# Cache pages: the page numbers of the next group are loaded into registers ahead of the wait for its ring slot

## The chip, the cores and the metric

The kernel runs on one core of one Trainium2 chip. The metric is the time of one execution on the device in microseconds (us); the kernel before takes 1488.07 us, the median of three runs from 1487.55 to 1489.52. A profile is one more execution, recorded instruction by instruction, with a time of its own.

## The reference

It is one step of a decoder layer: a half-step SwiGLU feed-forward network (ffa), a mixing block, a second feed-forward network (ffb), a layer norm after each. 512 prompt tokens and 8 decoding sequences of one token each go through the same weights. The part that matters here is the attention of the 8 decoding tokens over their past, which lies in a paged cache. A table of page numbers says which pages belong to which sequence:

```python
k_past = cache_k[l][page_table].reshape(DB, past, DA_HEADS, 2, DA_QK)
v_past = cache_v[l][page_table].reshape(DB, past, DA_HEADS, DA_V)
lp = jnp.einsum('bqhmd,bkhmd->bhmqk', q, k_past)       # logits of the past
attn = p[:, :, 0] - lam * p[:, :, 1]                   # two softmax maps per head
o = jnp.einsum('bhqk,bkhe->bqhe', attn[..., :P], v_past) + ...
```

Eight sequences with 16 pages of 128 positions each give 128 pages of keys and 128 pages of values. A page is 128 rows of 512 float32 values, 256 KB. The same block also holds the prompt's attention and an RWKV-7 recurrence (projections, triangular inverses, state products), which is other work for the same engines.

## The kernel before

The instructions of every engine are written out by hand, and semaphores order them. TensorE (PE), VectorE (DVE), ScalarE (ACT) and GpSimd (POOL) compute. SyncE (SP) issues nearly all DMA transfers, in the order of its program, and everything behind a wait on SP waits too.

The mixing block interleaves three strands on TensorE: the prompt's attention, the RWKV-7 work and the decoding tokens' pages. The pages come in 64 groups of GROUP = 4: groups 0 to 31 (N_GROUPS = 32) are keys, groups 32 to 63 are values. A key group is used by `decode_keys_tensor` (matmuls of L1063, four of 128x512), a value group by `decode_values_tensor` (L1126). Both first wait for all four pages of the group, and signal `pages_used` with their last matmul. Their places between the other matmuls are fixed.

The buffers are a ring of RING_GROUPS = 2 slots, `cache_pages0` and `cache_pages1`. `page_group(k)` on SP fills slot k % 2. From group 2 on it first waits until TensorE has used group k - 2, which lay in that slot. For each of the four pages it then loads the page number from the table in SBUF (`TABLE`, in profiles `page_ids`) into a register of SP with `value_load` (L1962: the instructions TENSOR_LOAD, FUSED_REGOPS and SEQ_ASSERT) and issues the transfer whose address is computed from it (L1964: FUSED_REGOPS, MOVE and DMA_DIRECT2D). Four loads and four issues thus alternate, all behind the wait. Between page groups SP also issues the last blocks of the input projection's weights (`input_block`, L1971), the outputs `v_out` (L2006), `k_out` (L2009) and `shift_out` (L2013), and one block of weights behind group 28 (L2018). Behind group 63, SP waits for the end of the mixing block and streams the weights of the output projection (L239) and of ffb.

ACT issues a few transfers of its own: 256 KB pieces of the recurrent state, in (L1640) and out (L1633).

Of the kernel before, what the change touches and what calls it, by code (L numbers as in the profile page):

```python
# [16 lines left out]
D_MODEL, SEQ, DEC = 1024, 512, 8  # L17
# [10 lines left out]
PAGES = PAST // PAGE  # L28
POOL = 160
# [28 lines left out]
GROUP, RING_GROUPS = 4, 2  # L58
# [53 lines left out]
def layer(nc, x_in, gu_a, down_a, w_in, w_out, gu_b, down_b, consts, vecs, lams, lora, g2,  # L112
# [17 lines left out]
    with ctx:  # L130
        def sb(name, shape, dt=f32, to=ctx):
            return to.enter_context(nc.sbuf_tensor(name, shape, dt))

        def sem(name):
            return ctx.enter_context(nc.semaphore(name))
# [58 lines left out]
        TABLE = sb("page_ids", [1, DEC * PAGES], i32)  # L194
# [13 lines left out]
        def g(name):  # L208

            if name not in sems:  # L210
                sems[name] = sem(name)
            return sems[name]
# [21 lines left out]
        def load_weights(sp, pr, i, src):  # L234
            for b, (k0, nk, _, _, _) in enumerate(pr.body):

                wait_from_one(sp, split_lo, 2 * (pr.block(i, b) - 1))
                slot = pr.raw_slot(b)
                sp.dma_start(RAW[slot][:, 0:nk, :], src(i, b)).then_inc(raw_ready[slot], 16)  # L239
# [37 lines left out]
        def multiply_woven(pe, slabs, seq, hi, lo, ready):  # L277

            order, seen = [], {}
            for n, (k, t) in enumerate(seq):  # L280
                pr, i, b = slabs[k]
                _, nk, sets, _, _ = pr.body[b // 2]
                s, slot = sets[b % 2], pr.slot(b)
                if k not in seen:
                    seen[k] = 0
                    pe.wait_ge(split_lo, pr.slab(i, b) + 1)
                    wait_from_one(pe, acc_free[s], pr.set_uses(i, b))
                if t not in order:
                    order.append(t)
                    pe.wait_ge(ready[0], ready[1] + len(order))  # L290
                seen[k] += 1
                for m, (w, x) in enumerate(((WH, hi), (WH, lo), (WL, hi))):
                    for a in range(2):
                        mm = nc.tensor.matmul(acc[s][:, a, 0:HALF], w[slot][:, t, :], x[:, t, HALF * a:HALF * a + HALF],  # L294
                                              start=seen[k] == 1 and m == 0, stop=seen[k] == nk and m == 2)
                if seen[k] == nk:
                    mm.then_inc(slab_used, 1)
# [331 lines left out]
        N_LEVELS = len(LEVELS) - 1  # L629
        JOBS = ring_order()  # L630
        JOB_AT = {name: n for n, (name, _, _) in enumerate(JOBS)}
        READER = {name: reader for name, reader, _ in JOBS}
        READS, FIRST_BANK, BEFORE = {}, {}, {}
        reads, at, holds = {"v": 0, "s": 0}, 0, [None] * 4
        for name, reader, banks in JOBS:
            reads[reader] += 1
            READS[name] = reads[reader]
            if banks == 2 and at % 2:
                at = (at + 1) % 4
# [4 lines left out]
            at = (at + banks) % 4  # L644
# [382 lines left out]
        N_GROUPS = QUARTERS * DEC  # L1027
# [910 lines left out]
        def _(sp):  # L1938
# [10 lines left out]
            def down(w):  # L1949
# [3 lines left out]
                        .rearrange("a p (k n) -> p (a k) n", n=2 * P)  # L1953
                return src

            def page_group(k):
                if k >= RING_GROUPS:
                    sp.wait_ge(g("pages_used"), k - RING_GROUPS + 1)
                slot, v = k % RING_GROUPS, k - N_GROUPS
                for n in range(GROUP):  # L1960
                    at = k % DEC * PAGES + k // DEC * GROUP + n if v < 0 else (2 * n + v % 2) * PAGES + v // 2
                    pid = sp.value_load(TABLE[0:1, at:at + 1], min_val=0, max_val=POOL - 1)  # L1962
                    cache = cache_k if v < 0 else cache_v
                    sp.dma_start(PG[slot][:, n, :], cache[bass.ds(pid, 1), :, :].rearrange("a p n -> (a p) n"))\  # L1964
                        .then_inc(g(f"pages_in{slot}"), 16)

            def input_block(n):
                pr, i, k = slab_of(2 * n)
                wait_from_one(sp, split_lo, 2 * (pr.block(i, k // 2) - 1))
                slot = pr.raw_slot(k // 2)  # L1970
                sp.dma_start(RAW[slot][:, :, :], w_in[ORDER[n][0] // 2, :, :].rearrange("p (k n) -> p k n", n=2 * P))\  # L1971
                    .then_inc(raw_ready[slot], 16)
# [21 lines left out]
            for n in range(6, 11):  # L1994
                input_block(n)
            sp.wait_ge(g("table_in"), 16)
            page_group(0)
            page_group(1)
            input_block(11)
            page_group(2)  # L2000
            input_block(12)
            page_group(3)
# [209 lines left out]
```

## Time and profile before

| | |
|---|---|
| median of three runs | 1488.07 us (1487.55 to 1489.52) |
| the profiled execution: its time, its span | 1481.32 us, 1479.5 us |
| TensorE busy, VectorE, ScalarE, GpSimd | 88%, 37%, 28%, 6% of the span |
| first page issued, last page group used | 534.5 us, 952.6 us from the span's start |
| page transfers | 256 of 256 KB, 3.0 us each from issue to landing |

The span is the time from the first to the last instruction of the program in the profile. Times inside the profile are counted from its start. PE is a matmul, PEld the load of its stationary operand; SPq are instructions of SP's sequencer. "Landing" is the moment at which the transfer's semaphore has its full count. A wait on an engine is counted as idle time in front of the instruction that waits.

### The profile page before, as it was taken

What the parts mean: (1) busy time and instruction counts of PE and PEld (TensorE: products, weight loads), DVE (VectorE), ACT (ScalarE), POOL (GpSimd) and SP (SyncE); (2) the same over time, 40 slices, a digit from 0 to 9 for tenths busy, and PEclk for the clock granted to TensorE, in tenths of its full rate; (3) what the DMA queues carried; (4) which work ended last, traced back from release to release, by engine and by line L of the source; (5) the groups of instructions that cost most, each with busy time, mean ns of one, the idle gap of its engine ahead of it and who ended that gap; (6) DMA issues with size and microseconds to landing.
All of it is one profiled execution on the core that took longest, in us unless ns stands there. A gap on an engine that the chain in (4) does not pass through costs nothing.

```text
span 1479.5 us, 30154 instructions
## 1 busy us (share of the span) xinstructions
PE 1296.7 (88%) x12636; PEld 1161.2 (78%) x12636; DVE 554.0 (37%) x787; ACT 421.1 (28%) x637; POOL 94.8 (6%) x92
## 2 busy tenths in 40 slices
PE   6999999999969977977768777779699999999995
PEld 6999999999958976854436334369599999989994
DVE  3332332223364552235522423275633333322224
ACT  4322222211234521126612313132332222221113
POOL 0000000000100021002410001002000000000000
PEclk9999999999979989999978889789899999999998
DMA  5222222223225233664574567533122322213211
GB/s 201 86 92 107 85 85 71 79 79 96 80 95 196 78 128 105 204 197 138 166 218 142 169 205 213 179 151 136 58 86 86 109 88 85 78 57 100 78 57 58
DMA packets 55963, 174.62 MB, mean 118 GB/s; under 512 B 7105, under 2 KB 7362, under 8 KB 47298
## 3 DMA queue, kind: packets, MB, share of 16 engines
q1 hardware_dynamic: 53282, 168.84, 34.2%
q10 hardware_dynamic: 2592, 4.52, 0.8%
q8 instruction: 64, 1.05, 0.3%
q14 instruction: 25, 0.20, 0.0%
HBM read 163.58 MB, written 9.76 MB: 117 GB/s over the span
## 4 chain that ended last, share of the span: by engine, by line
PE 37%; DVE 5%; DMA 4%; SPq 4%; ACT 3%; issue 2%; DVEq 0%; ACTq 0%
PE acc L271 26%; DMA cache_pages<-in_cache_v 2%; SPq L1962 2%; SPq L1964 2%; PE acc L294 2%; PE acc L1126 1%; PE acc L391 1%; DMA x_lo<-trunk_lo 1%; DVE weights_lo L254 1%; PE acc L717 1%; PE acc L1294 1%; PE acc L1397 1%; PE acc L1063 1%; PE acc L1317 1%; PE acc L1200 1%
## 5 line engine op out<-in xcount | busy, mean ns | idle before, releaser
L254 DVE TENSOR_TENSOR weights_lo<-weights_raw,weights_hi 128x1024 fp32r<-128x1024 f32 (+2 forms) x186 | 207.1, 1122 | 525.1 <-ACT weights_hi L247 525.0
L271 PE MATMUL acc<-x_hi,weights_hi 128*128 128x260 f32 x1728 | 354.1, 286 | 17.3 <-DVE x_lo L2079 11.6
L271 PE MATMUL acc<-x_lo,weights_hi 128*128 128x260 f32 x1728 | 350.6, 285 | 0.0
L271 PE MATMUL acc<-x_hi,weights_lo 128*128 128x260 f32 x1728 | 350.6, 285 | 0.0
L247 ACT ACTIVATE weights_hi<-weights_raw 128x1024 fp32r<-128x1024 f32 (+2 forms) x186 | 178.5, 966 | 593.7 <-PE acc L271 558.3
L271 PEld LDWEIGHTS acc<-x_hi,weights_hi 128*128 128x128 f32 x1728 | 270.2, 191 | 26.4 <-issue 25.7
L271 PEld LDWEIGHTS acc<-x_hi,weights_lo 128*128 128x128 f32 x1728 | 269.1, 190 | 0.0
L271 PEld LDWEIGHTS acc<-x_lo,weights_hi 128*128 128x128 f32 x1728 | 268.9, 190 | 0.0
L271 PE MATMUL acc<-hidden_hi,weights_hi 128*128 128x260 f32 x704 | 144.3, 287 | 12.4 <-DVE weights_lo L254 12.4
L271 PE MATMUL acc<-hidden_hi,weights_lo 128*128 128x260 f32 x704 | 143.5, 285 | 0.0
L271 PE MATMUL acc<-hidden_lo,weights_hi 128*128 128x260 f32 x704 | 143.4, 286 | 0.0
L271 PEld LDWEIGHTS acc<-hidden_hi,weights_hi 128*128 128x128 f32 x704 | 110.4, 192 | 13.2 <-issue 13.2
L271 PEld LDWEIGHTS acc<-hidden_lo,weights_hi 128*128 128x128 f32 x704 | 110.6, 191 | 0.0
L271 PEld LDWEIGHTS acc<-hidden_hi,weights_lo 128*128 128x128 f32 x704 | 110.4, 191 | 0.0
L1126 PE MATMUL acc<-cache_pages,query_columns 128*8 128x512 f32 x256 | 40.6, 711 | 30.6 <-DMA cache_pages<-in_cache_v 30.5
L322 ACT ACTIVATE hidden_hi<-scratch 128x520 f32 (+1 forms) x44 | 28.1, 639 | 101.8 <-DVE scratch L333 101.8
L1063 PE MATMUL acc<-cache_pages,query_columns 128*32 128x512 f32 x256 | 38.9, 684 | 15.1 <-DMA cache_pages<-in_cache_k 13.7
L404 POOL TENSOR_TENSOR scratch<-y_sum 128x520 f32<-128x520 f32 x3 | 4.8, 1591 | 725.5 <-DVE y_sum L350 725.5
L336 DVE TENSOR_TENSOR hidden_lo<-scratch,hidden_hi 128x520 f32 (+1 forms) x44 | 30.8, 700 | 38.9 <-ACT hidden_hi L322 38.9
L333 DVE TENSOR_TENSOR scratch<-scratch,acc 128x520 f32<-128x520 f32 x44 | 30.3, 689 | 33.3 <-PE acc L271 33.3
L347 DVE SCALAR_TENSOR_TENSOR y_sum<-x_hi,acc 128x520 f32 (+1 forms) x24 | 16.6, 691 | 62.9 <-PE acc L271 57.7
L391 PE MATMUL acc<-scratch,mean_weights 128*128 128x260 f32 x96 | 30.1, 482 | 11.0 <-ACT scratch L416 11.0
(286 smaller groups left out, 1302.8 us busy)
## 6 DMA issues: line engine op xcount, KB each, us to landing
cache_pages<-in_cache_k SPq DMA_DIRECT2D x128, 256.0 KB, 3.0
cache_pages<-in_cache_v SPq DMA_DIRECT2D x128, 256.0 KB, 3.0
weights_raw<-in_gate_up_a SPq DMA_DIRECT2D x22, 1024.0 KB, 4.8
weights_raw<-in_gate_up_b SPq DMA_DIRECT2D x22, 1024.0 KB, 4.8
weights_raw<-in_w_in SPq DMA_DIRECT2D x13, 1024.0 KB, 4.8
weights_raw<-in_down_a SPq DMA_DIRECT2D x8, 768.0 KB, 4.2
weights_raw<-in_down_b SPq DMA_DIRECT2D x8, 768.0 KB, 4.2
weights_raw<-in_down_a SPq DMA_DIRECT2D x8, 640.0 KB, 3.8
```

The lines of the kernel that those rows point to most:

```text
L247: nc.scalar.activation(WH[pr.slot(k)][:, 0:nk, :], RAW[slot][:, 0:nk, P * (k % 2):P * (k % 2) + P], ACT.Copy).then_inc(split_hi, 1)
L254: nc.vector.tensor_tensor(WL[pr.slot(k)][:, 0:nk, :], RAW[slot][:, 0:nk, P * (k % 2):P * (k % 2) + P], WH[pr.slot(k)][:, 0:nk, :].bitcast( ...
L271: mm = nc.tensor.matmul(acc[s][:, a, 0:HALF], w[slot][:, t, :], x[:, k0 + t, HALF * a:HALF * a + HALF], start=begins and t == tiles[0] and ...
L294: mm = nc.tensor.matmul(acc[s][:, a, 0:HALF], w[slot][:, t, :], x[:, t, HALF * a:HALF * a + HALF], start=seen[k] == 1 and m == 0, stop=see ...
L322: nc.scalar.activation(HH[:, bass.ds(2 * (i - 1) + k - 2, 1), :], SCR[:, k:k + 1, :], ACT.Copy).then_inc(h_hi, 1)
L333: dve.tensor_tensor(halves(SCR[:, k, :]), halves(SCR[:, k - 2, :]), accv(k), ALU.mult).then_inc(hidden, 1)
L336: dve.tensor_tensor(HL[:, bass.ds(c, 1), :], SCR[:, k:k + 1, :], HH[:, bass.ds(c, 1), :].bitcast(f32), ALU.subtract).then_inc(acc_free[k], 1)
L391: mm = nc.tensor.matmul(acc[1][:, a, 0:HALF], MEAN[:, :], SCR[:, 2 + c % 2, HALF * a:HALF * a + HALF], start=c == 0, stop=c == DC - 1)
L1063: mm = nc.tensor.matmul(bank(DECODE_BANK)[32 * h:32 * h + 32, :], QZ[:, h, b, :], PG[k % RING_GROUPS][:, :, P * h:P * h + P], start=b == 0 ...
L1126: mm = nc.tensor.matmul(bank(DECODE_BANK)[32 * j:32 * j + 8, :], WZ[:, n, 8 * b:8 * b + 8], PG[k % RING_GROUPS][:, j, :], start=False, sto ...
L1962: pid = sp.value_load(TABLE[0:1, at:at + 1], min_val=0, max_val=POOL - 1)
L1964: sp.dma_start(PG[slot][:, n, :], cache[bass.ds(pid, 1), :, :].rearrange("a p n -> (a p) n"))\
```

## The change

`page_group(k)` no longer loads page numbers between its transfers. A new helper, `page_ids(k)`, loads the four numbers of group k into four registers and keeps them in the Python dictionary `ids`. `page_group(k)` waits for its slot, issues four transfers in a row from the registers kept, and then calls `page_ids(k + 1)`. So the loads of a group stand in SP's program behind the transfers of the group before it, ahead of whatever SP does between the two groups. Group 0 loads its own numbers first. After group 63 nothing is loaded.

```diff
+            ids = {}
+
+            def page_ids(k):
+
+                v = k - N_GROUPS
+                at = [k % DEC * PAGES + k // DEC * GROUP + n if v < 0 else (2 * n + v % 2) * PAGES + v // 2 for n in range(GROUP)]
+                ids[k] = [sp.value_load(TABLE[0:1, n:n + 1], min_val=0, max_val=POOL - 1) for n in at]
+
             def page_group(k):
+                if k not in ids:
+                    page_ids(k)
                 if k >= RING_GROUPS:
                     sp.wait_ge(g("pages_used"), k - RING_GROUPS + 1)
-                slot, v = k % RING_GROUPS, k - N_GROUPS
-                for n in range(GROUP):
-                    at = k % DEC * PAGES + k // DEC * GROUP + n if v < 0 else (2 * n + v % 2) * PAGES + v // 2
-                    pid = sp.value_load(TABLE[0:1, at:at + 1], min_val=0, max_val=POOL - 1)
-                    cache = cache_k if v < 0 else cache_v
+                slot, cache = k % RING_GROUPS, cache_k if k < N_GROUPS else cache_v
+                for n, pid in enumerate(ids.pop(k)):
                     sp.dma_start(PG[slot][:, n, :], cache[bass.ds(pid, 1), :, :].rearrange("a p n -> (a p) n"))\
                         .then_inc(g(f"pages_in{slot}"), 16)
+                if k + 1 < 2 * N_GROUPS:
+                    page_ids(k + 1)
```

The number of instructions of SP is the same, 1095 rows of the program before and after, and no other engine's program changes. In the lists below, one row is one instruction or several equal ones; "ISA" rows are SP's register instructions, and lines below L1962 have moved: L1964 of before is L1971 of after, and L1971 of before is L1980 of after.

Before, on SP, at group 3 (behind the last block of the input projection's weights), the wait for the slot stands ahead of the first load:

```order
L1971 DMA weights_raw<-in_w_in 128x2048 [waits split_lo]
L1962 TENSOR_LOAD page_ids [waits pages_used]
L1962 ISA x2
L1964 ISA
L1964 DMA cache_pages<-in_cache_k 128x512
L1962 TENSOR_LOAD page_ids
L1962 ISA x2
L1964 ISA
L1964 DMA cache_pages<-in_cache_k 128x512
```

After, on SP, at the same place, the last of group 3's four loads stands ahead of the weights, and the wait stands ahead of four transfers with no load between them:

```order
L1962 TENSOR_LOAD page_ids
L1962 ISA x2
L1980 DMA weights_raw<-in_w_in 128x2048 [waits split_lo]
L1971 ISA [waits pages_used]
L1971 DMA cache_pages<-in_cache_k 128x512
L1971 ISA
L1971 DMA cache_pages<-in_cache_k 128x512
L1971 ISA
L1971 DMA cache_pages<-in_cache_k 128x512
L1971 ISA
L1971 DMA cache_pages<-in_cache_k 128x512
L1962 TENSOR_LOAD page_ids
```

The wait has moved from a load to the first instruction of a transfer, and four loads that stood behind it now stand ahead of it.

Before, on SP, the start of the stretch, where group 0 needs no slot and waits only for the table:

```order
L1962 TENSOR_LOAD page_ids [waits table_in]
L1962 ISA x2
L1964 ISA
L1964 DMA cache_pages<-in_cache_k 128x512
L1962 TENSOR_LOAD page_ids
```

After, on SP, the same place:

```order
L1962 TENSOR_LOAD page_ids [waits table_in]
L1962 ISA x2
L1962 TENSOR_LOAD page_ids
L1962 ISA x2
L1962 TENSOR_LOAD page_ids
L1962 ISA x2
L1962 TENSOR_LOAD page_ids
L1962 ISA x2
L1971 ISA
L1971 DMA cache_pages<-in_cache_k 128x512
```

Here the first transfer has moved behind three more loads.

## Rows read from the trace of the kernel before

**Rows 1.** The page of the profile: busy tenths in 40 slices of the span.

```profile
PE   6999999999969977977768777779699999999995
...
DMA  5222222223225233664574567533122322213211
```

**Rows 2.** Waits of TensorE (PE) on pages: us in total, times, longest.

```profile
PE acc L1063 <- DMA cache_pages<-in_cache_k: 13.7, 6, 4.7
...
PE acc L1126 <- DMA cache_pages<-in_cache_v: 30.5, 16, 4.9
```

**Rows 3.** The chain that ended last, 740 to 953 us, by line.

```profile
by line: DMA cache_pages<-in_cache_v 15.4%; SPq L1962 14.9%; SPq L1964 12.1%; issue 10.9%; PE acc L1126 10.1%; PE acc L1397 3.9%; PE acc L1104 3.5%; DMA cache_pages<-in_cache_k 2.7%; PE acc L1317 2.7%; PE acc L1294 2.5%; PE acc L1063 2.3%; 
```

**Rows 4.** The same chain, pieces in order of time: start us, us, what.

```profile
756.70 2.78 DMA cache_pages<-in_cache_k
...
881.88 0.27 SPq L1962
882.60 0.33 SPq L1964
...
885.86 2.92 DMA cache_pages<-in_cache_v
888.83 1.04 PE acc L1126 x8
...
944.06 2.70 DMA cache_pages<-in_cache_v
```

**Rows 5.** Timeline of TensorE: its wait for the pages of six groups, in brackets.

```profile
647.66 0.73 PE L1063 MATMUL acc<-cache_pages,query_columns 128*32 128x512 f32 x4 [4.73 <-DMA cache_pages<-in_cache_k]
...
806.47 1.04 PE L1126 MATMUL acc<-cache_pages,query_columns 128*8 128x512 f32 x8 [0.89 <-DMA cache_pages<-in_cache_v]
...
828.25 1.23 PE L1126 MATMUL acc<-cache_pages,query_columns 128*8 128x512 f32 x8 [2.99 <-DMA cache_pages<-in_cache_v]
...
865.54 1.04 PE L1126 MATMUL acc<-cache_pages,query_columns 128*8 128x512 f32 x4 [4.90 <-DMA cache_pages<-in_cache_v]
...
903.72 1.60 PE L1126 MATMUL acc<-cache_pages,query_columns 128*8 128x512 f32 x8 [3.28 <-DMA cache_pages<-in_cache_v]
...
942.51 1.90 PE L1126 MATMUL acc<-cache_pages,query_columns 128*8 128x512 f32 x8 [2.09 <-DMA cache_pages<-in_cache_v]
```

**Rows 6.** L1962, L1964, L1063: duration ns min/median/max, first and last start us.

```profile
L1962 SPq TENSOR_LOAD <-page_ids x256: 262/268/967, 533.6 to 947.7; - x128
L1962 SPq FUSED_REGOPS  x256: 152/152/177, 534.1 to 948.0; - x128
L1962 SPq SEQ_ASSERT  x256: 18/18/33, 534.3 to 948.2; - x128
...
L1964 SPq FUSED_REGOPS  x256: 37/37/42, 534.4 to 948.3; - x128
...
L1063 PE MATMUL acc<-cache_pages,query_columns x256: 589/617/1062, 562.0 to 769.5; 128*32 128x512 f32 x128
...
L1964 SPq MOVE cache_pages<-in_cache_k x128: 29/29/38, 534.5 to 765.4; - x128
```

**Rows 7.** Timeline of SP: a run of 12 page issues, start us, us.

```profile
753.43 12.40 SPq L1964 DMA_DIRECT2D cache_pages<-in_cache_k  x12
```

**Rows 8.** SP's waits for slots, 862 to 953 us: total, times, longest.

```profile
SPq L1962 <- PE acc L1126: 5.9, 7, 2.0
```

**Rows 9.** The page of the profile: issues, KB each, us to landing.

```profile
cache_pages<-in_cache_v SPq DMA_DIRECT2D x128, 256.0 KB, 3.0
weights_raw<-in_gate_up_a SPq DMA_DIRECT2D x22, 1024.0 KB, 4.8
```

**Rows 10.** DMA packets of 534 to 542 us, then of 920 to 950 us.

```profile
DMA packets 881, 2.42 MB, mean 302 GB/s; under 512 B 95, under 2 KB 95, under 8 KB 751
...
DMA packets 3743, 6.88 MB, mean 229 GB/s; under 512 B 416, under 2 KB 416, under 8 KB 3738
```

**Rows 11.** L1962's loads from 594 to 606.5 us, beside the stores of k and v.

```profile
L1962 SPq TENSOR_LOAD <-page_ids x8: 265/450/967, 595.1 to 605.7; - x8
```

**Rows 12.** Stretch 939 to 944 us: busy us of the engines, clock, DMA share, GB/s.

```profile
939.00:944.00 5.00, 2.91 (x20) 0.63 (x16) 0.50 (x2) 0.00 (x0) 0.00 (x0) 0.50 0.81 255
```

## The prediction

> **What bounds the kernel now.** I read the page first. TensorE is busy at 9 tenths over most of the span, and dips to 6 to 8 tenths only in the middle, where the mixing block runs and where the DMA engines are busiest [rows 1]. The rest of the kernel is feed-forward networks, which the change doesn't touch. So the question is what TensorE waits for in the middle.
>
> The list of waits says that 44.2 us of its idle time end with the landing of a page: 13.7 us in 6 waits for key pages and 30.5 us in 16 waits for value pages [rows 2]. Idle time counts only where it lies on the path, so I then read the chain of work that ended last. From 740 to 953 us, 18.1% of the chain is page transfers, and 27.0% is SP loading numbers and issuing (14.9% and 12.1%) [rows 3]. Of 213 us that is 57.5 us; a group shows in these two lines with about 4 x 0.84 = 3.35 us (below), so some 17 groups stand on the chain with their whole issuing. The transfers stand on it 12 times, the first at 756.70, the last at 944.06 us [rows 4]. Before 740 us the chain has no page piece: there it runs through ScalarE, VectorE and TensorE.
>
> One passage shows the pattern: TensorE has used a group, SP loads the first number at 881.88, issues the fourth page at 885.86, the page lands 2.92 us later, and TensorE goes on at 888.83 [rows 4]. From the free slot to the use it is 6.95 us, of which 3.98 us lie before the fourth issue.
>
> **The change part by part.** *The spacing on SP.* Twelve issues in a row take 12.40 us, the last being 0.33 long, so one page costs SP (12.40 - 0.33) / 11 = 1.10 us, and a group 4.4 us [rows 7]. The load part is 268 + 152 + 18 = 438 ns [rows 6], the issue part 37 + 29 + 333 = 399 ns, of which 333 ns are the transfer's own instruction [rows 4, 6]. The two sum to 837 ns, so 260 ns are gaps between six instructions, 43 ns each. With three gaps each, a load costs 0.57 us and an issue 0.53 us.
>
> *After the change* the first issue starts 0.14 us behind the free slot (37 + 29 ns and gaps) and not 0.72, and the fourth at 0.14 + 3 x 0.53 = 1.73 us and not 3.98. The four loads, 2.3 us, come behind. Where SP then waits for a slot anyway, they are hidden; where it doesn't, a group still costs it 4.4 us. The change takes nothing off SP's work: it moves the issues to the front of SP's turn.
>
> *How much of this the landing keeps.* Four pages issued within 1.6 us are 1 MB at once. Pages have never been issued so closely in the trace, so I bound it. From below: one weight transfer of 1,024 KB lands 4.8 us after its issue [rows 9], which gives 0.14 + 4.8 = 4.9 us behind the free slot. From above: at the mean 229 GB/s of the late stretch [rows 10] a page of 262 KB takes 1.14 us, and the fourth lands at 0.14 + 3.0 + 3 x 1.14 = 6.6 us. But that rate is one of pages issued 1.1 us apart, so it may only be what was asked for. Where page transfers met a weight transfer in flight, the rate was 302 GB/s [rows 10], 0.87 us a page; a weight transfer that comes alone moves its last 768 KB in 4.8 - 3.0 = 1.8 us, 0.60 us a page [rows 9]. I take 0.75, between these two: 0.14 + 3.0 + 2.25 = 5.4 us. Against 6.95 us that is **1.5 us per passage**, with ends of 0.35 and 2.0.
>
> The Trainium skill ("DMA: Bandwidth & Descriptors", section "Latency and other measured facts") gives a floor of about 600 ns for a load of a register from a tensor. The trace disagrees: the median of 256 loads is 268 ns [rows 6]. By the page the four loads would take 1.3 us more out of the path and a passage would shrink by up to that much more; by the row the sum stays as it is.
>
> *How many passages.* A wait can give back no more than it has, and in a stretch where SP's 4.4 us per group set the pace the earlier issue is gained once, not per group. In order of time: the end of the keys (748 to 769 us, five waits in a row) once, 1.5; the wait of 0.89 us at 806.47, 0.9; the wait of 2.99 at 828.25, 1.5; one near 843 us, 1.5; 4.90 at 865.54, 1.5; the run of three from 880 to 889, once, 1.5; 3.28 at 903.72, 1.5; and the last stretch, from 924 to 952, once, 1.5 [rows 5]. That is 7 x 1.5 + 0.9 = 11.4 us. In the last 91 us SP waited only 5.9 us in all [rows 8], so no more than about 5.9 + 1.5 us can come from there; I count 4.5.
>
> *The group at 647.66* waited 4.73 us [rows 5], as its pages landed late among transfers of states that ScalarE issues. There the four issues now come before those. Up to 3 us are gained at that point, but before 740 us the chain runs through other engines, so I let 0.6 us of it last. The sum is **12 us**.
>
> *What else moves.* The four loads of the next group now stand ahead of whatever SP does between two groups: two blocks of the input projection's weights, the stores of v, k and the last rows, one block of weights behind group 28. None of these comes later for it, since the turn before them lost as many loads as it got. Only group 0 has four loads more than it had in its turn: its first page is issued 3 x 0.57 = 1.7 us later, its fourth at the same time (4 x 0.57 + 1.73 = 4.0 us), and SP reaches the weights behind group 1 some 2.3 us later. TensorE uses the first page at 562.0 [rows 6], 27 us behind the first issue of before, and the weights wait for VectorE's signal anyhow. If both covers were gone it would cost 2.3 us once. The new wait stands ahead of the transfers; behind it is nothing but SP's own program, as before. Behind group 63 nothing is loaded, so the output projection's weights come no later.
>
> Against its own execution the sum is 1481.32 - 12 = 1469.3 us. That execution was 6.75 us faster than the median, so for the median I take 1488.07 - 12 = **1476 us**.
>
> **The rivals.** *A. The transfers set the landing.* If four pages at once get no more than the 229 GB/s of the late stretch [rows 10], a passage gains 0.35 us and 8 to 9 of them give 3 us: 1485 us. For it: the DMA engines are busy 0.81 of the time at 939 to 944 us, with 255 GB/s [rows 12]. Against it: the 302 GB/s, and weight transfers that land 1 MB in 4.8 us. The Trainium skill ("DMA: Bandwidth & Descriptors", section "Bandwidth") has a transfer of 1 MB, issued from GpSimd, at 6.15 us; by that page a passage would take 0.14 + 6.15 = 6.3 us and the sum would be about 5.5 us; the row of 4.8 us disagrees with it for this kernel.
>
> *B. Other engines take over.* What TensorE no longer waits for pages it waits for ScalarE and VectorE, as it does before 740 us. If only half of the passages last, 6 us remain: 1482 us. Against it: 45% of the chain from 740 us on is SP and pages, and the steps between two passages are mostly TensorE's own [rows 3]. What is late next at these places is TensorE's own matmuls.
>
> *C. It gets slower: the loads behind four transfers are long.* The longest load took 967 ns, and the eight from 594 to 606.5 us have a median of 450 ns, against 268 [rows 11]. Each long one stood behind a page issue while a store of k or v was in flight. If four transfers in a row have this effect on the loads behind them, SP's turn grows, and it counts at each of the some 17 groups on the chain. It is even with the gain at 12 / 17 = 0.7 us per group. With two loads of each group as long as the worst there, some 1.0 us per group, it is 17 - 12 = +5 us: 1493 us. Against it: the other loads stood behind page issues too, with up to three pages in flight, and stayed at 268 ns; the long ones stood beside stores, which read SBUF.
>
> *D. More than forecast.* TensorE's clock stands at 0.50 of full, its lower level of 1.2 GHz, from 939 to 944 us, and a group's matmuls take 1.90 us there [rows 5, 12] against 1.04 us elsewhere. Up to then TensorE had been idle in 2 of 5 us. If the shorter waits bring the clock back for six groups, that is 6 x 0.86 = 5 us more: 1471 us.
>
> **How the numbers follow.** Forecast 0.60, A 0.11, B 0.12, C 0.08, D 0.09. The forecast's own ends are its passages at 1.1 and 1.9 us: 1479 and 1472 us. About 0.2%, 3 us, is what a measurement can tell from no change, so faster means below 1485.1. That holds for the forecast, for B, for D and for a few of A's cases: 0.82. A's others and the mild cases of C are the same: 0.11. Slower is 0.07. The range takes in D with a somewhat faster transfer, 1468, and B and A up to 1485; outside are C above and 1 in 10 at the lower end.
>
> **What would show it.** In the changed profile, four issues stand 0.53 us apart, four loads behind them are still at 268 ns with a turn of 4.4 us where SP doesn't wait, and the fourth page lands 5.4 us behind the slot's release. TensorE's waits for pages fall from 44 to about 30 us, and SP's loads are gone from most of the chain. The median time from issue to landing must rise above 3.0, since pages queue behind each other; if it rises to about 4.2 for the fourth, A has come true. I am wrong if the loads grow (C), or if TensorE's waits shrink and the time doesn't (B).

## The result, and the profile after

The changed kernel takes 1480.09 us, the median of five runs (1475.03 to 1483.22), against 1489.07 us before (five runs, 1487.55 to 1490.58). The ratio is 0.9933, with a 95% interval of 0.9913 to 0.9953. It is faster by 9.0 us where 12 were forecast, and 1480.09 lies in the range of 1468 to 1485.

The two profiled executions say the opposite: 1483.22 us for the changed kernel, the slowest of its five runs, and 1481.32 us for the kernel before, which is faster than every run of it that was timed without a profile. So each kernel was profiled once more among the experiments (after_again, 1473.44 us; before_again, 1486.31 us). Below, a main reading counts only if both profiles of a kernel show it.

The page of the changed kernel, busy tenths in 40 slices, beside [rows 1]:

```profile
PE   6999999999969977978768768688699999999995
...
DMA  5222222223225233654564566533122322213211
```

TensorE's dips in the middle are still there: of the 40 slices six differ, three of them by a tenth up and three down.

TensorE's waits for pages in the changed kernel, as in [rows 2] (us in total, times, longest):

```profile
PE acc L1126 <- DMA cache_pages<-in_cache_v: 29.9, 15, 3.5
...
PE acc L1063 <- DMA cache_pages<-in_cache_k: 10.2, 3, 4.2
```

The total is 40.1 us, and 38.4 in the second profile; it was 44.2, and 46.0 in the second profile of the kernel before. What has shrunk most is the longest wait for values: 4.9 and 4.7 us in the two profiles before, 3.5 in both now.

SP's instructions for the page groups, from the list of the changed kernel's tiles and lines, beside [rows 6] and [rows 9] (duration ns min/median/max, first and last start in us; then us from issue to landing):

```profile
L1962 SPq TENSOR_LOAD <-page_ids x256: 260/266/936, 532.7 to 945.1; - x128
...
L1971 SPq DMA_DIRECT2D cache_pages<-in_cache_k x128: 332/333/2621, 535.3 to 766.2; - x128
...
DMA to landing us min/median/max: 2.5/3.5/6.6
```

The loads are as long as before. The transfers take longer from issue to landing, 3.5 us for 3.0, since four of them now stand in the queues together.

One passage of the changed kernel, from the chain that ended last (start us, us, what):

```profile
897.43 1.02 PE acc L1126 x8
...
898.61 0.33 SPq L1971
899.13 0.33 SPq L1971
899.68 0.33 SPq L1971
900.20 0.33 SPq L1971
...
900.88 0.27 SPq L1962
```

TensorE's last matmul on the old group ends at 898.45. The four issues follow, 0.52 to 0.55 us apart, and the loads for the next group stand behind them. The fourth issue is 1.75 us behind the free slot; in [rows 4] it took 3.98 us. The fourth page landed at 904.28 and TensorE went on at 904.32, 5.9 us behind the free slot where [rows 4] have 6.95 (counted there from the first load).

The chain of the changed kernel from 740 to 953 us, by line, first and second profile:

```profile
by line: SPq L1971 12.4%; DMA cache_pages<-in_cache_v 12.3%; issue 10.9%; PE acc L1126 9.2%; SPq L1962 8.4%; PE acc L1309 5.5%; PE acc L1294 4.5%; PE acc L1397 4.3%; PE acc L1317 4.0%; PE acc L1104 3.5%; PE acc L1063 2.9%; PE acc L1200 2.2%
```

```profile
by line: SPq L1971 16.2%; SPq L1962 12.2%; issue 10.5%; DMA cache_pages<-in_cache_v 10.1%; PE acc L1126 8.0%; PE acc L1317 4.0%; PE acc L1294 3.9%; PE acc L717 3.5%; PE acc L1104 3.5%; PE acc L1397 3.0%; PE acc L1284 2.3%; PE acc L1200 2.2%
```

Value transfers stood on the chain with 15.4% [rows 3], 14.1% in the second profile of before, and stand there with 12.3 and 10.1%. But SP's loads are still on it, with 8.4 and 12.2%.

### The profile page after: what moved, and what is told of

The parts are those of the page before. It is cut to its first block, busy times and chain, and to the rows that moved or that the text cites. A ratio compares the mean times of both kernels' runs of the same rounds, so it can differ in the third digit from the quotient of the medians.

```text
span 1481.4 us, 30154 instructions
## 1 busy us (share of the span) xinstructions
PE 1301.0 (88%) x12636; PEld 1166.8 (79%) x12636; DVE 554.5 (37%) x787; ACT 422.0 (28%) x637; POOL 94.1 (6%) x92
## 4 chain that ended last, share of the span: by engine, by line
PE 77%; DVE 7%; ACT 5%; DMA 4%; issue 3%; SPq 3%; ACTq 0%; DVEq 0%
PE acc L271 61%; PE acc L294 3%; SPq L1971 2%; DMA cache_pages<-in_cache_v 2%; PE acc L1063 2%; PE acc L391 2%; DVE weights_lo L254 1%; PE acc L717 1%; PE acc L1126 1%; SPq L1962 1%; PE acc L1317 1%; PE acc L1294 1%; DMA x_lo<-trunk_lo 1%; PE acc L1309 1%; PE acc L1397 1%
## 5 line engine op out<-in xcount | busy, mean ns | idle before, releaser
L1063 PE MATMUL acc<-cache_pages,query_columns 128*32 128x512 f32 x256 | 38.6, 678 | 11.6 <-DMA cache_pages<-in_cache_k 10.2
```

What stands on the lines that cost most here:

```text
L1063: mm = nc.tensor.matmul(bank(DECODE_BANK)[32 * h:32 * h + 32, :], QZ[:, h, b, :], PG[k % RING_GROUPS][:, :, P * h:P * h + P], start=b == 0 ...
```

## The experiments

The theory L: a passage through a free slot got shorter by what the fourth landing got earlier, and apart from that SP's turn per group (4.4 us, unchanged) still sets the pace. The rivals are those of the prediction, above all B (other engines take over, so how far the loads are moved makes no difference) and A (the transfers alone set the landing). In some of the expectations, theory B is another one: that issues close to each other are what counts. Theory C is there a gain that lies in TensorE's clock or in chance stops.

Five measures come from the traces by one rule. Over the groups in which SP waited for the slot, the time runs from the end of the last matmul on the slot's old group to the first issue, the fourth issue and the fourth landing; the table has the medians. They are over the groups whose first issue directly follows that end (18 to 52 of them). Most of these groups are key groups; the value groups alone give 7.12 and 7.25 us for the fourth landing in the two profiles before (18 and 19 groups), 5.87 and 6.18 with the change (9 each). SP's turn is the lower quartile of the times from a value group's first issue to the next one's. In most kernels that is a group where SP didn't wait, and the shortest turns are within 0.02 us of it. In the three kernels without the range check SP waits at most groups and the quartile is too long: the shortest turns are 3.23 us in no_assert_before, 3.26 in no_assert and 2.95 in multi_load.

The ratio is that of a kernel to the kernel before as it ran beside it, whose median was 1486.99, 1488.62 or 1489.14 us.

| kernel | ratio to before (95%) | slot to 1st issue | to 4th issue | to 4th landing | turn |
|---|---|---|---|---|---|
| before, again | 1.0015 (0.9996 to 1.0035) | 0.78 | 4.04 | 7.18 | 4.37 |
| the change, again | 0.994 (0.992 to 0.9961) | 0.21 | 1.76 | 6.16 | 4.29 |
| one_ahead | 0.9953 (0.9936 to 0.997) | 0.20 | 3.47 | 6.53 | 4.35 |
| two_ahead | 0.9933 (0.9907 to 0.9959) | 0.21 | 2.91 | 6.31 | 4.35 |
| no_assert_before | 0.9912 (0.988 to 0.9945) | 0.50 | 2.92 | 6.66 | 3.65 |
| no_assert | 0.988 (0.986 to 0.99) | 0.20 | 1.76 | 6.13 | 3.32 |
| double_loads | 1.0101 (1.008 to 1.0122) | 0.21 | 1.76 | 6.14 | 5.38 |
| half_before | 0.9919 (0.9894 to 0.9944) | 0.77 | 4.04 | 6.25 | 4.37 |
| half_after | 0.9837 (0.9814 to 0.9861) | 0.21 | 1.76 | 4.15 | 4.29 |
| multi_load | 0.9874 (0.9842 to 0.9906) | 0.20 | 1.75 | 6.23 | 3.46 |

All times are us. The first profiles of the two kernels give 7.03 (before) and 6.05 (after) for the fourth landing.

### How far ahead: one number, two, all four

In each of these kernels a function `ahead(k)` says how many of a group's four numbers are loaded behind the transfers of the group before it. The others are loaded between the transfers, as before.

```diff
-                for n, pid in enumerate(ids.pop(k)):
+                for n in range(GROUP):
+                    pid = ids.pop((k, n)) if (k, n) in ids else page_id(k, n)
```

one_ahead has `return 1`:

> Only the first of the next group's four numbers is loaded ahead of the wait; the other three are loaded between the transfers, as before. SP's turn is as long as before. Theory L (what counts is the time from the free slot to the landing of the fourth page): the first issue comes 0.57 us earlier, the fourth too (at 3.4 us in place of 4.0), the fourth page lands 0.6 us earlier, and nine passages give 5 us: ratio 0.9965. Theory B (close issues are what helps, or hurts): spacing is unchanged at 1.1 us, so nothing: 1.000. Theory C (the gain is in TensorE's clock or in when executions happen to stall): no order between this run, the one with two ahead and the full change.

Measured: 1479.97 us, ratio 0.9953 (0.9936 to 0.997). two_ahead has `return 2`:

> Two of the four numbers are loaded ahead. Theory L: the fourth issue comes at 2.9 us behind the free slot; with 2.9 us to land it would be there at 5.8 us, and as the transfers themselves held the fourth page to about 6.0 us in the full change, this has nearly all of the full gain: 8 us, ratio 0.9945. If instead the gain grows with each load moved, half of it: 0.9965. Theory B: a third of the full gain, since two of the issues are close.

Measured: 1474.61 us, ratio 0.9933 (0.9907 to 0.9959).

The fourth landing moves step by step, from 7.0 or 7.2 us to 6.5, 6.3 and then 6.05 or 6.16 us with all four ahead. The time moves with it at first. L had expected 0.9965 and 0.9945; both lie in the intervals, and so one number ahead can't be told from what L expected, nor two ahead from four. That only close issues count (1.000 for one number ahead) is excluded. The fourth issue counts less than its own shift: from two to four ahead it comes 1.15 us earlier (2.91 to 1.76), but the landing only 0.15 to 0.26 us. By then the pages queue behind each other, as the half pages below show.

### Keys or values

values_only has `return 0 if k < N_GROUPS else 4`:

> The numbers are loaded ahead for the value groups (32 to 63) alone; the key groups are as before. Theory L: seven of the nine passages lie there, so about 6.5 to 7 us of the 9: ratio 0.9955. If the gain is the group at 647 us, where the states come in between, or the end of the keys, this run shows under 3 us: 0.998 or more.

Measured: 1480.94 us, ratio 0.9955 (0.9938 to 0.9973), as expected. keys_only has `return 4 if k < N_GROUPS else 0`:

> The numbers are loaded ahead for the key groups (0 to 31) alone. Theory L: two of the nine passages, and the value groups alone had 6.5 us: 2 us, ratio 0.9985. If it has more than 4 us, the parts don't add up, and the gain of the value groups alone must have had another source.

Measured: 1489.15 us, ratio 0.9993 (0.9974 to 1.0012): nothing that can be told from no change, though a gain up to 3.9 us is inside the interval, and so are the 2 us of L. The two halves multiply to 0.9948, which is in the intervals of the whole. The gain that can be measured is in the values.

### SP's turn, shorter and longer

no_assert loads the numbers without the check of their range, so FUSED_REGOPS and SEQ_ASSERT (152 + 18 ns and their gaps) go, four times per group; no_assert_before does the same with no number ahead.

```diff
-                ids[k] = [sp.value_load(TABLE[0:1, n:n + 1], min_val=0, max_val=POOL - 1) for n in at]
+                return sp.value_load(TABLE[0:1, at:at + 1])
```

> As the changed kernel, with the numbers loaded without the check that they lie in range (two instructions less per page): SP's turn goes from 4.35 to about 3.3 us. This leaves out the check only. Theory L with SP as the pace of the late stretches: beyond the change's gain another 3 to 4 us, ratio 0.991. If the transfers are the pace (1 MB needs 5.8 us to land and two groups overlap), a shorter turn brings nothing: 0.994 as the change.

> The order of before (load, issue, load, issue, all behind the wait), with the numbers loaded without the check of their range. This leaves out the check only. SP's turn is 3.3 us, the fourth issue comes at about 2.85 us behind the free slot. Theory L with the pace: the fourth page lands at about 5.8 to 6.0 us, as in the changed kernel, and the turn is as short as in the run with the change and no check; so it has the gain of that run, or 1 to 2 us less: ratio 0.989. Theory B (close issues, loads out of the way of the wait): without moved loads it has only what the shorter turn gives, that is the difference between that run and the change: 0.995.

Measured: 1469.30 us, ratio 0.988 (0.986 to 0.99), and 1477.19 us, ratio 0.9912 (0.988 to 0.9945). A turn that is 1.0 us shorter (the shortest ones are 4.28 and 3.26 us) gains 8 to 9 us beyond the change (0.9933 or 0.994 to 0.988), where 3 to 4 were expected: this was a miss by size. The two edits together give more than the change alone. Whether they give more than no_assert_before, or less than the product of the two single ratios (0.9853), can't be told: the interval of no_assert_before is 0.0033 wide to each side. It takes in L's 0.989 and, just, not the 0.995 of the theory of close issues. Now SP goes partly off the chain. The chain of no_assert from 740 to 938 us, by line, and SP's waits for slots with values:

```profile
by line: DMA cache_pages<-in_cache_v 12.5%; SPq L1978 11.7%; PE acc L1126 10.6%; issue 9.7%; PE acc L1309 7.0%; PE acc L1317 4.3%; SPq L1964 3.8%; PE acc L1294 3.8%; PE acc L1104 3.7%; PE acc L1063 3.7%; PE acc L1397 3.0%; PE acc L1284 2.5%
```

```profile
SPq L1978 <- PE acc L1126: 52.8, 17, 21.5
```

Loads (L1964 there) and issues (L1978) fall to 15.5% together, against 20.8 and 28.4% in the two profiles of the change. SP waits for TensorE in 17 groups of values; with the change alone it waits in 9 and 7.

double_loads goes the other way: two loads more per group, whose numbers nobody uses, behind the transfers.

```diff
                 if k + 1 < 2 * N_GROUPS:
                     page_ids(k + 1)
+                    for n in range(2):
+                        page_id(k + 1, n)
```

> The changed kernel with two more loads of a number, unused, behind each group's four: SP's turn is 5.5 us in place of 4.35, the issues and the landings stay as in the change. Theory L with SP as the pace: at some 17 groups the turn is on the path, so 17 x 1.14 = 19 us are lost and 9 gained: ratio 1.007. If the turn hides behind TensorE and only the landing counts, it stays at 0.994.

Measured: 1502.69 us, ratio 1.0101 (1.008 to 1.0122). That is slower than before the change, though the fourth page lands 6.14 us behind the free slot, as early as with the change. Its chain from 740 to 972 us, and SP's waits for slots with values from 795 to 970 us:

```profile
by line: SPq L1964 30.3%; SPq L1978 23.1%; issue 16.5%; DMA cache_pages<-in_cache_v 5.1%; PE acc L1104 3.2%; PE acc L1126 2.6%; DMA cache_pages<-in_cache_k 1.8%; PE acc L1397 1.6%; PE acc L1063 1.3%; PE acc L1294 1.3%; PE acc L1284 1.3%; PE
```

```profile
SPq L1978 <- PE acc L1126: 21.3, 2, 16.7
```

SP waits in 2 groups only, and 53.4% of the chain is SP. From the change (0.994) to this kernel (1.0101) are 24 us for a turn that is 1.09 us longer: it counts about 22 times. L had expected 17 times and 1.007, which is just outside the interval, on the side of too little. So L's second half holds: where TensorE waits for SP's turn, the turn's length counts. That moving loads within such a turn gives nothing is argued; no kernel has the long turn in the order of before.

### Half of each page

half_before and half_after move only 256 of the 512 columns of each page (the first two groups apart), in the order of before and of the change. TensorE's matmuls are the same. The other half of the slot keeps older data, so these two kernels leave out half of the past and return wrong values for it; they are for measuring only. Of the edit, the line of the transfer:

```diff
+                    sp.dma_start(PG[slot][:, n, 0:512 if k < 2 else 256], cache[bass.ds(pid, 1), :, 0:512 if k < 2 else 256].rearrange("a p n -> (a p) n"))\
```

> Each page transfer from group 2 on brings only the first 256 of the 512 columns; the other half of the slot keeps older data, so the attention over the past is computed from wrong values, with the same matmuls. Order of before. The transfers are half as large, so the fourth lands perhaps 0.3 us earlier; SP's turn and spacing are as before. Theory L: the fourth issue at 4.0 us sets the landing, so hardly anything is gained: 2 to 4 us, ratio 0.998.

> The same half pages with the changed order: the fourth issue comes 2.25 us earlier than in the half pages of before. Theory L with transfers that hold the fourth page back: now nothing holds it, so nine passages keep 2 us and not 0.95: 17 to 19 us against before, ratio 0.988. If the spacing of the landings (1.2 us from the second to the third and from the third to the fourth) comes from something else than the amount of data, a fixed time per transfer for example, it stays at 0.993.

Measured: 1475.48 us, ratio 0.9919 (0.9894 to 0.9944), and 1462.51 us, ratio 0.9837 (0.9814 to 0.9861). Both were misses by size. The first was expected to gain 2 to 4 us, since its issues are 1.1 us apart as before; it gains 12, as each transfer is some 0.8 us shorter by itself. The list of tiles has it for half_before:

```profile
DMA to landing us min/median/max: 1.9/2.2/4.4
```

So a passage ends 0.8 to 0.9 us earlier there, and gains like the change without any change of order. The second was expected to gain 17 to 19 us and gains 24. Its fourth page lands 2.9 to 3.0 us earlier than before, so the gain is about 8 us for each us, against some 9 in the change. The medians of the landings of pages 1 to 4, behind the first issue of their group:

| kernel | 1st | 2nd | 3rd | 4th |
|---|---|---|---|---|
| before | 2.96 | 4.06 | 5.26 | 6.29 |
| after | 2.79 | 3.57 | 4.74 | 5.86 |
| the change, again | 2.77 | 3.60 | 4.70 | 5.95 |
| half_before | 2.19 | 3.25 | 4.39 | 5.48 |
| half_after | 2.17 | 2.73 | 3.28 | 3.99 |

With whole pages, issued 0.53 us apart, the third and the fourth land 1.10 to 1.25 us behind the one before. With half pages they land 0.55 and 0.71 us apart, little more than their issues. Nothing differs but the size, so in the change the fourth landing is set by the transfers' size, and no longer by SP's spacing alone. Whether it is the bytes or the size of the packets isn't told apart: a half page has rows of 1 KB where a whole one has 2 KB.

### The two kernels again

> The changed kernel once more, on the chip of this call, and for a second profile. Theory L: 0.993 to 0.994. In its profile TensorE's waits for pages are below those of before; the idle pieces of TensorE that no wait explains (6 pieces over 0.9 us, 10.1 us, against 3 with 3.6 us in the first pair of profiles) are of single executions and are at 3 to 6 pieces here too.

> The kernel before against itself: 1.000, with an interval that shows what five rounds can tell. Its first profile was of an execution of 1481 us, faster than all timed ones (1483 to 1494); this one should be near 1487, with more unexplained idle pieces or a lower clock of TensorE than the first.

Measured: 1477.49 us, ratio 0.994 (0.992 to 0.9961), and 1487.92 us, ratio 1.0015 (0.9996 to 1.0035). With their profiles the pair can be compared along its length. From TensorE's first page group to its last it is 396.9 us in before_again and 385.6 us in after_again; the first profiles had 390.7 and 392.0. The waits of TensorE for three value groups in before_again, from its timeline:

```profile
845.87 1.90 PE L1126 MATMUL acc<-cache_pages,query_columns 128*8 128x512 f32 x8 [3.70 <-DMA cache_pages<-in_cache_v]
...
865.82 1.89 PE L1126 MATMUL acc<-cache_pages,query_columns 128*8 128x512 f32 x8 [4.65 <-DMA cache_pages<-in_cache_v]
...
942.05 1.89 PE L1126 MATMUL acc<-cache_pages,query_columns 128*8 128x512 f32 x8 [4.63 <-DMA cache_pages<-in_cache_v]
```

and for the same groups in after_again:

```profile
841.64 1.90 PE L1126 MATMUL acc<-cache_pages,query_columns 128*8 128x512 f32 x8 [2.86 <-DMA cache_pages<-in_cache_v]
...
860.41 1.04 PE L1126 MATMUL acc<-cache_pages,query_columns 128*8 128x512 f32 x8 [3.50 <-DMA cache_pages<-in_cache_v]
...
937.20 1.90 PE L1126 MATMUL acc<-cache_pages,query_columns 128*8 128x512 f32 x8 [3.15 <-DMA cache_pages<-in_cache_v]
```

The waits are 0.84, 1.15 and 1.48 us shorter, which is about the size of the earlier landing (1.0 us). The second group also runs its eight matmuls in 1.04 us and not 1.89: TensorE's clock is back at 2.4 GHz there. In after_again 10 of the 64 groups take over 1.5 us for their matmuls, that is, they run mostly at the lower clock of 1.2 GHz; in before_again it is 16 (11 and 14 in the first profiles).

Where the first profile of the changed kernel lost its gain shows on its TensorE, against the kernel before, long before the values. The timeline of after:

```profile
663.32 0.33 PE L1294 MATMUL acc<-inverse,t_turned 64*64 64x64 f32 x4 [1.94 <-issue]
```

and the stretches from 660 to 670 us, of after and then of before (us, busy us of PE, PEld, DVE, ACT, POOL, granted clock, DMA share, GB/s):

```profile
660.00:670.00 10.00, 7.18 (x94) 5.16 (x94) 2.35 (x4) 2.77 (x4) 0.00 (x0) 0.69 0.10 32
```

```profile
660.00:670.00 10.00, 7.66 (x194) 5.79 (x194) 4.42 (x8) 4.50 (x7) 0.00 (x0) 1.00 0.40 119
```

TensorE stopped for 1.94 us with no wait on another engine or a page, and the mean clock of the stretch is 0.69 and not 1.00. Two key groups that are 10.6 us apart before came 14.6 us apart here. In after_again the same stop is 1.35 us long and they are 12.0 us apart. Stops over 0.9 us that the profile calls "issue" add up, in the mixing block, to 3.6 and 6.2 us in the two profiles before and 10.1 and 7.4 us with the change.

These stops are not accidents of single executions. In all 14 profiles they stand before the same seven matmuls of TensorE's program; one takes 0.94 us every time, and the other six vary from nothing to 2.5 us. What comes in front of those six shows among the DMA packets, from 660.9 to 662 us of after:

```profile
q8 instruction: 1, 0.02, 5.1%
```

This is one packet of 16 KB on a queue for instructions, from 660.98 to 661.88 us, and TensorE goes on at 663.32. In each of the 48 stops over 0.9 us at the six places, such a packet ended 1.0 to 1.6 us before TensorE went on. So TensorE most likely waits there for its own next instructions; no run holds this apart from other causes.

Does the change make these stops longer? Three of the six places are in the stretch of the keys (663, 750 and 755 us). Together they take 5.8 and 3.6 us in the two profiles of the change, and 4.0 to 4.9 in the other four kernels that issue four whole key pages at once. In the eight profiles that don't, they take 0.5 to 2.9 us (1.0 and 2.5 before). At the three places in the stretch of the values there is no such difference (3.4 and 3.7 us with the change, 3.5 and 4.0 before). This is a likely reason why keys_only gains nothing, but it isn't shown: behind its stops before_again waits for key pages anyway, and no run changes the stops alone.

### One load for four numbers

multi_load builds on the change and reads a group's four numbers with one load into four registers (a row of four for keys, every 32nd number for values), without the check of their range.

```diff
-                ids[k] = [sp.value_load(TABLE[0:1, n:n + 1], min_val=0, max_val=POOL - 1) for n in at]
+                _, ids[k] = nc.values_load_multi_w_load_instructions(
+                    these, engines=[sp.engine if hasattr(sp, "engine") else sp], min_val=0, max_val=POOL - 1,
+                    skip_runtime_bounds_check_because="the page table holds numbers of the pool")
```

> As the changed kernel, with one load instruction for the four registers of a group (the four numbers lie at one spacing in the table) and without the check of their range, which is all that is left out. SP's turn falls from 4.35 to between 2.5 us (a load costs the same for four registers) and 3.3 us (200 ns and more for each). Theory L with the pace: at least the gain of the run without the check, ratio 0.985 to 0.988. If the landing (5.9 us) and TensorE's own use of the slot now set the pace, nothing beyond 0.988.

Measured: 1468.99 us, ratio 0.9874 (0.9842 to 0.9906), the same as no_assert within their intervals. The list of the load's line, for all, then up to 767.5 us (the keys' numbers), then from there to 940 us (the values'):

```profile
L1966 SPq TENSOR_LOAD <-page_ids x64: 295/850/984, 534.1 to 932.9; - x64
...
L1966 SPq TENSOR_LOAD <-page_ids x32: 295/301/984, 534.1 to 764.5; - x32
...
L1966 SPq TENSOR_LOAD <-page_ids x32: 849/862/877, 768.0 to 932.9; - x32
```

The median of all is misleading, as there are two kinds of loads. Four numbers that lie side by side take 301 ns, hardly more than one (266 ns). Four that lie 32 apart in the table take 862 ns. So the load that this kernel needs where the gain is, among the values, is the slow kind. SP's turn there is 2.95 us where it doesn't wait, 0.3 us shorter than in no_assert (3.26). That gives nothing that can be measured: of the 31 value turns SP doesn't wait in only 4 (6 in no_assert), and the fourth page lands no earlier. These two are the best of the versions that compute the right result. Both give up the range check of the page numbers.

## Why the prediction was right, and where it was off

**What bounds the kernel** was read rightly: the slot's passage and SP's turn. Lengthening the turn with the landing left alone costs 24 us, and moving the landing with the turn left alone gains 9 (the change) and 12 (half_before).

**The spacing on SP** was right to a few hundredths. The first issue comes 0.21 us behind the slot (0.14 said), the fourth 1.76 (1.73), the loads stay at 266 ns, and the turn is 4.29 us (4.4).

**How much of it the landing keeps** is the term that was mis-sized. The prediction took 0.75 us per page and so 5.4 us from the free slot to the landing, a gain of 1.5 us per passage. Measured are 6.05 and 6.16 us, and a gain of 1.0. The 229 GB/s of the late stretch [rows 10] were dismissed as "what was asked for". In the burst from 879 to 883 us of after_again, and while pages come 1.1 us apart from 883 to 889 us of before_again, the packets give:

```profile
DMA packets 564, 1.02 MB, mean 256 GB/s; under 512 B 64, under 2 KB 64, under 8 KB 564
```

```profile
DMA packets 804, 1.47 MB, mean 245 GB/s; under 512 B 87, under 2 KB 87, under 8 KB 804
```

A burst gets hardly more than the spaced transfers did, 256 KB in 1.02 us. The weights' 4.8 us for 1 MB [rows 9] was the wrong neighbour. The Trainium skill ("DMA: Bandwidth & Descriptors", section "Bandwidth") has 6.15 us for one transfer of 1 MB issued from GpSimd; the prediction said that the row of 4.8 us disagrees with it for this kernel. For a burst of four pages the measurement comes near the figure of the Trainium skill, though it is another kind of transfer and counted otherwise: the fourth page lands 5.86 and 5.95 us behind the first issue.

**Rival A** was therefore half true. The transfers do set the fourth landing, as half_after shows (4.15 us in place of 6.16). But a page costs the gap of 1.0 to 1.2 us only behind the second page, where A had it for all three; the second page costs 0.8 us. And the first lands 2.8 us behind its issue, not 3.0. So the passage gained 1.0 us and not 0.35, and the time is not A's 1485.

**How many passages**: with 1.0 us in the place of 1.5, the prediction's own places give 7 x 1.0 + 0.9 + 0.6 = 8.5 us, and 9.0 were measured. That near agreement is in part luck, as the places were not all right. The end of the keys was counted once, and the group at 647.66 us at 0.6 us; keys_only gives 1.0 us in all (a gain of 3.9 to a loss of 1.8), so these 2.1 us are neither shown nor excluded. That group still waits 4.19 and 4.08 us, where it was 4.73 and 5.04. The stops for instructions, which are longer in the keys' stretch with the change, were no term of the sum. The values' own places make 6 x 1.0 + 0.9 = 6.9 us, and values_only measured 6.7 (0.9955 of 1488). Some of it may not be waits but clock: 10 or 11 groups ran at the low clock where it was 14 or 16, and at 0.86 us each these are 3 to 5 us. That is **rival D**'s mechanism at other places than it named. No kernel holds the clock apart from the waits, so this share is argued and not shown, and single places of the sum could be less than they seem.

**Rival B** had the waits shrink and half of it lost to other engines, 1482 us. No run bears it out. The gain per us of earlier landing is about as large at 2.9 us (half_after, 24 us) as at 1.0 us (the change, 9), so half of it isn't lost to other engines. **Rival C** did not come for the loads: the longest took 936 and 982 ns (967 and 1212 before) and the median did not move. It was the page issues that were held up more often, as the last section says. Its price was right all the same, and even low: double_loads shows that SP's turn counts at about 22 groups, where 17 were said (that is with SP still more on the chain than in the change).

**What would show it**: of its signs, the issues, the loads and the turn came true. TensorE's waits fell to 40.1 and 38.4 us, not to about 30, since the landing gained less. "SP's loads are gone from most of the chain" was wrong, and by the prediction's own words it had to be: the change takes nothing off SP's work, and where the turn sets the pace the loads stand on the chain wherever in the turn they are. Loads and issues together had 27.0 and 26.6%, and have 20.8 and 28.4%.

## What to carry to other kernels

A wait for a buffer should have nothing behind it that doesn't need the buffer; but what is moved ahead of it stays in the queue's turn, so first see whether the queue waits for the consumer (a gain per passage) or the consumer for the queue (only a shorter turn helps). Here the range check, 1.0 to 1.1 us of the turn, gave as much as the whole reordering when it was left out.

When issues are brought together, the size of the gain is set by how far apart the landings stay. Take that from transfers of the same shape in the same stretch, not from ones with longer rows elsewhere.

A median over instructions of one line can mix two kinds. Look at minimum and maximum, and split the list by stage, before working out a price per item.

Where single executions scatter by as much as the change brings, profile both kernels twice before reading a cause out of one pair. Where a stop has no cause in the list of waits, see whether it stands before the same instruction in every profile, and what the queues for instructions did just before.

## What the runs showed of the hardware

- Four registers loaded by one instruction of SP take 301 ns where the four numbers lie side by side (median of 32 loads), and 862 ns where they lie 32 apart in their table (32 loads). One register takes 266 ns.
- The range check of a loaded number costs SP 152 + 18 ns in its two instructions, and with gaps 1.0 to 1.1 us per group of four (shortest turns 4.28 against 3.26 us, and 4.35 against 3.23). Leaving it out gains as much again as the change.
- Issues that follow each other at 0.53 us are held up more often. Of 256 page issues on SP, whose median is 333 ns, 4 and 3 took over 0.6 us in the two profiles of the kernel before, 13 and 17 with the change, 7 in one_ahead and 17 in half_after; the longest took 2.62 us with the change and 1.09 before. What all issues took beyond 333 ns each sums to 2.6 and 3.0 us before and to 11.0 and 12.7 us with the change. Since half pages issued as closely have as many, it goes with how closely transfers are issued and not with their bytes. The cause isn't known. The medians of the table don't show these pieces; they may take back some of the gain, which no run shows.
- In a burst of transfers of 256 KB in rows of 2 KB the second lands 0.8 us behind the first, and the third and fourth 1.1 to 1.25 us behind the one before, though they are issued 0.53 us apart. Pages issued 1.1 us apart land 1.0 to 1.2 us apart. Halves of pages, issued 0.53 us apart, land 0.55 to 0.7 us apart.
- TensorE stops for up to 2.5 us at six places of its program, the same in all 14 profiles. Each of the 48 stops over 0.9 us ended 1.0 to 1.6 us after a packet of 16 KB on a queue for instructions.
